# First weight unit and input brought and split in interleaved pieces, in a two-layer hybrid decoder step

## What is computed

```python
x = x + 0.5 * swiglu(rmsnorm(x, norm_ffn1), ffn1_gate, ffn1_up, ffn1_down)
proj = rmsnorm(x, norm_mix) @ w_in        # columns split into 4 head groups
x = x + concat(rwkv7, rglru, gated_delta_net, gla) @ w_out
x = x + 0.5 * swiglu(rmsnorm(x, norm_ffn2), ffn2_gate, ffn2_up, ffn2_down)
```

## Time and profile before

| what | value |
|---|---|
| median of three timed runs | 1355.63 us (1355.2 to 1355.84) |
| profiled execution, first to last instruction (span) | 1353.3 us |
| TensorE busy | 1328.3 us, 98% of the span |
| VectorE busy | 855.3 us, 63% |
| ScalarE busy | 692.1 us, 51% |
| granted TensorE clock, mean of the core | 0.999 |
| first matmul | 7.46 us after the span's start |

### The profile page before, as it was taken

The page is one execution under the profiler, slowest core; times in us unless marked ns, Lnnn a source line. Parts: engine busy times, 40 slices in busy tenths (PEclk is TensorE's granted clock), DMA queues, the critical chain, the costliest instruction groups (busy, mean ns, idle before and its releaser), DMA issues.

```text
span 1353.3 us, 31424 instructions
## 1 busy us (share of the span) xinstructions
PE 1328.3 (98%) x12584; PEld 1288.1 (95%) x12584; DVE 855.3 (63%) x1327; ACT 692.1 (51%) x995; POOL 77.6 (6%) x113
## 2 busy tenths in 40 slices
PE   7999999999999999999999999999999999999997
PEld 7999999998888999999999999999888899999997
DVE  6656533898876756653376555349988767555533
ACT  6554423757565654443365444347466655444423
POOL 0000000200030100000010000001001310000001
PEclk9999999999999999999999999999999999999999
DMA  8544455322313644444455444443222244544541
GB/s 294 175 147 147 148 155 151 114 79 80 112 50 110 203 153 142 153 155 145 150 189 154 154 141 154 145 151 109 80 79 97 66 158 155 155 148 146 155 141 54
DMA packets 50769, 185.90 MB, mean 137 GB/s; under 512 B 5761, under 2 KB 6273, under 8 KB 50177
## 3 DMA queue, kind: packets, MB, share of 16 engines
q1 hardware_dynamic: 49104, 177.37, 41.5%
q10 hardware_dynamic: 1584, 7.35, 1.5%
HBM read 180.14 MB, written 4.56 MB: 136 GB/s over the span
## 4 chain that ended last, share of the span: by engine, by line
PE 83%; DVE 11%; ACT 3%; issue 2%; DMA 1%; POOL 0%; DVEq 0%; ACTq 0%; POOLq 0%
PE ps L479 26%; PE ps L481 25%; PE ps L480 25%; DVE wl L1592 2%; DVE ar L1749 2%; PE ps L847 1%; DVE ar L1663 1%; PE ps L749 1%; DMA raw<-wts 1%; PE ps L1035 0%; PE ps L1013 0%; DVE ar L1740 0%; ACT ar L1299 0%; ACT wh L1186 0%; PE ps L817 0%
## 5 line engine op out<-in xcount | busy, mean ns | idle before, releaser
L479 PE MATMUL ps<-xh,wh 128*128 128x320 f32 x1952 | 611.2, 313 | 8.2 <-DVE xl L1614 8.2
L1592 DVE TENSOR_TENSOR wl<-raw,wh 128x1024 fp32r<-128x1024 f32 x332 | 407.9, 1230 | 318.1 <-ACT wh L1186 317.8
L481 PE MATMUL ps<-xh,wl 128*128 128x320 f32 x1952 | 603.8, 309 | 0.0
L480 PE MATMUL ps<-xl,wh 128*128 128x320 f32 x1952 | 603.8, 309 | 0.0
L1186 ACT ACTIVATE wh<-raw 128x1024 fp32r<-128x1024 f32 x332 | 349.1, 1054 | 355.6 <-PE ps L481 339.0
L479 PEld LDWEIGHTS ps<-xh,wh 128*128 128x128 f32 x1952 | 367.0, 188 | 19.1 <-issue 9.0
L480 PEld LDWEIGHTS ps<-xl,wh 128*128 128x128 f32 x1952 | 367.2, 188 | 0.5
L481 PEld LDWEIGHTS ps<-xh,wl 128*128 128x128 f32 x1952 | 367.1, 188 | 0.0
L479 PE MATMUL ps<-hid_h,wh 128*128 (+1 forms) x704 | 217.5, 309 | 0.0
L480 PE MATMUL ps<-hid_l,wh 128*128 (+1 forms) x704 | 217.5, 309 | 0.0
L481 PE MATMUL ps<-hid_h,wl 128*128 (+1 forms) x704 | 217.5, 309 | 0.0
(11 more groups left out here) (290 smaller groups left out, 935.2 us busy)
## 6 DMA issues: line engine op xcount, KB each, us to landing
raw<-wts SPq DMA_DIRECT2D x332, 512.0 KB, 3.5
ms<-mst ACTq DMA_DIRECT2D x2, 1440.0 KB, 7.6
mout<-ms ACTq DMA_DIRECT2D x2, 1440.0 KB, 6.6
x<-xT SPq DMA_DIRECT2D x4, 320.0 KB, 4.8
yT<-x SPq DMA_DIRECT2D x4, 320.0 KB, 2.5
cs<-cst SPq DMA_DIRECT2D x1, 652.0 KB, 8.0
pr<-par ACTq DMA_DIRECT2D x1, 429.0 KB, 4.3
pr<-par ACTq DMA_DIRECT2D x1, 425.0 KB, 5.2
```

The costliest lines, as they stand in the source:

```text
L479: pe.matmul(out, a, rh, start=start, stop=False)
L480: pe.matmul(out, a, rl, start=False, stop=False)
L481: return pe.matmul(out, b, rh, start=False, stop=stop)
L1592: tt(wl[:, s, :], raw_of(layer, n), wh[:, s, :].bitcast(F32), ALU.subtract).then_inc(lo_ready.sem, 1)
```

## The change

The first weight unit is brought in two transfers (columns 0 to 255, then the rest) and split in three pieces (columns 0 to 255, 256 to 511, 512 to 1023), which stand among the tiles of the input on ScalarE and VectorE. The input comes in transfers of one, one, two and four tiles. TensorE's wait for `lo_ready` of unit 0 moves from its first block to its fifth. The first weight piece counts on the semaphore of the gains (`norms_in`), which ScalarE now awaits ahead of its first activation.

```diff
+        X_PIECES = (slice(0, 1), slice(1, 2), slice(2, 4), slice(4, 8))
...
             def load_x(s):
-                sp.dma_start(x[:, 2 * s:2 * s + 2, :], xT[:, 2 * s:2 * s + 2, :]).then_inc(x_in[s].sem, 16)
+                k = X_PIECES[s]
+                sp.dma_start(x[:, k, :], xT[:, k, :]).then_inc(x_in[s].sem, 16)
...
-            load(0)
-            for s in range(4):
-                load_x(s)
+            sp.dma_start(raw[:, 0, 0:256], wts[0, :, 0:256]).then_inc(norms_in.sem, 16)
+            load_x(0)
+            load_x(1)
+            sp.dma_start(raw[:, 0, 256:], wts[0, :, 256:]).then_inc(raw_in[0].sem, 16)
+            load_x(2)
+            load_x(3)
             load(1)
...
-                    if k == 0:
+                    if k == (0 if m else KT // 2):
                         pe.wait_ge(lo_ready.sem, layer * UNITS + base + m + 1)
...
-                split_hi(0, 0)
-                act.wait_ge(norms_in.sem, 16)
+                def first_hi(lo, hi):
+                    return act.activation(wh[:, 0, lo:hi], raw[:, 0, lo:hi], ACT.Copy)
+
+                act.wait_ge(norms_in.sem, 32)
+                first_hi(0, 256)
                 for k in range(KT):
-                    act.wait_ge(x_in[k // 2].sem, 16)
+                    if k == 2:
+                        act.wait_ge(raw_in[0].sem, 16)
+                        first_hi(256, 512)
+                    if k == 4:
+                        first_hi(512, 1024).then_inc(hi_ready.sem, 1)
+                    for s, piece in enumerate(X_PIECES):
+                        if k == piece.start:
+                            act.wait_ge(x_in[s].sem, 16)
                     act.activation(xh[:, k, :], x[:, k, :], ACT.Copy, scale=P("n1", k)).then_inc(xh_ready.sem, 1)
...
+                def first_low():
+                    for k in range(KT):
+                        ve.wait_ge(xh_ready.sem, k + 1)
+                        if k in (0, 2, 4):
+                            cols = slice(128 * k, 1024 if k == 4 else 128 * k + 256)
+                            if k == 4:
+                                ve.wait_ge(hi_ready.sem, 1)
+                            ins = tt(wl[:, 0, cols], raw[:, 0, cols], wh[:, 0, cols].bitcast(F32), ALU.subtract)
+                            if k == 4:
+                                ins.then_inc(lo_ready.sem, 1)
+                        stt(xl[:, k, :], x[:, k, :], P("n1", k), xh[:, k, :].bitcast(F32), ALU.mult, ALU.subtract).then_inc(xl_ready.sem, 1)
+
                 if layer == 0:
-                    split_lo(layer, 0)
-                    norm_low(layer, 0, "n1")
+                    first_low()
```

## The result

| | before | changed |
|---|---|---|
| median of 21 runs | 1354.94 us (1353.5 to 1356.37) | 1356.79 us (1354.82 to 1359.08) |
| profiled execution, span | 1353.3 us | 1355.1 us |

The ratio is 1.0012 (95% interval 1.0007 to 1.0018): the changed kernel is slower by 1.6 us, 0.9 to 2.4. That is less than 0.2%, but not no difference, and its sign is the opposite of the forecast one. With more runs the median before also lies 0.7 us under the one of three runs that the prediction started from.

A forecast was written before the change was run, and what follows sets the result against it. The prediction took TensorE's unbroken stretch of matmuls to bound the kernel. Unit 1 starting at 12.31 instead of 12.87 us wins 0.56 us, other effects cost nothing: 1355.63 - 0.56 = 1355.1 us, range 1353.9 to 1356.6.

The forecast's parts named there:

- What bounds the kernel: Whole execution: TensorE busy 98%, unbroken from its first matmul; only bringing that stretch forward helps, at most part of 7.46 us.
- First matmul at 5.7 to 6.7 us: TensorE's start: needing only a quarter unit, gains and tile 0, it begins 0.8 to 1.8 us sooner than 7.46.
- So the last byte of the input lands when it did: 2.60 + 5.3 = 7.9 us: Input load: same bytes ahead, engines at about 410 GB/s without a pause, so the landing time stays unchanged.
- slower transfers: Rival, loads at the start: shorter rows at half of 410 GB/s delay unit 1 by 1.1 us, 1356.2 us; chance 0.08.
- The chain from the landing: ScalarE and VectorE splits after input lands at 7.90 us: unit 1 starts on TensorE at 12.31 instead of 12.87.
- The clock: Rival, TensorE's start: holes keep the clock low, 1.75 us lost, 1356.8 us; chance 0.15.
- -0.56 as forecast: Start of unit 1 on TensorE: 12.31 us instead of 12.87, 0.56 us won for the whole execution.
- 0.03 for "slower": Whole kernel: chance 0.03 of measurably slower, from low clock and slow transfers together or an unseen program shift.
- The size against the whole: Whole kernel's time: every case stays within 0.2%, 2.7 us, told as no change; chance 0.95.
- The direction: Whole kernel's time: likeliest case is faster, 1355.63 to 1355.1 us; chance 0.62.

The follow-up runs named there:

- transfers-only runs: Changed kernel's transfers kept, unit 0 split whole ahead of the tiles as before; against the kernel before 1.0021 (first try, late table load) and 1.0014 (remade).
- the three variants: Changed kernel with input in four two-tile transfers (1.0003), first unit in one transfer (1.0005, then 0.9998), or tiles 0 and 1 issued from ScalarE's queue (1.0005).
- two queues: Changed kernel with input tiles 0 and 1 issued from ScalarE's queue instead of SP's; 1.0005 against the kernel before.
- holes filled: Changed kernel with 16 matmuls of zeros in each of its two holes, none ahead of the first matmul; 1.0032, again 1.002, against the kernel before.
- changed, filled: Changed kernel with 36 matmuls of zeros ahead of its first matmul and 16 in each of its two holes; 1.0015 against the kernel before.
- splits only: Changed kernel's splits in pieces, but unit 0 in one transfer and input in pairs as before; 0.9999 against the kernel before, in both tries.
- five fills: Matmuls of zeros added to the changed kernel (1.0015; holes alone 1.0032, 1.002), the kernel before (1.0011) and splits in pieces with the old transfers (1.0011).

## Why the prediction was wrong

*What bounds the kernel*: right. TensorE has no hole from the 25th matmul to 240 us, and that matmul is 1.75 us late for 1.6 us (0.9 to 2.4) by the medians. That the two profiled spans differ by 1.8 us as well is partly luck, since the spans of the changed kernel alone run from 1353.0 to 1357.3 us.

*First matmul at 5.7 to 6.7 us*: it came at 5.1. The chain of 1.9 us held; what it starts from, the gains and the first piece, was there at 3.15 instead of 4.75 us.

*"So the last byte of the input lands when it did: 2.60 + 5.3 = 7.9 us"*: **this step failed.** It landed at 9.5. The step took the 410 GB/s of the earlier trace rows for a property of the engines, whatever is queued. They were measured with 320 to 512 KB per issue of 0.47 us; with the 128 to 160 KB per issue of the change, which the issue rate holds to at most 160 KB / 0.47 us = 350 GB/s by this estimate, 245 GB/s flowed from 2.6 to 4.2 us for 396 before. The step also kept the issue time of before, 2.60 us, though the last input transfer is now sixth in the queue and issued at 3.08. I had slower transfers as a rival and priced them at 1.1 us, but looked for the cause in row length, which costs some 0.13 us, and gave it 0.08. The transfers-only runs show that the arrangement of the transfers makes the input late, and the three variants that larger transfers early in the queue, or a sooner issue of the large ones, mend it.

Of the 1.55 us, lost flow explains a part: 0.19 MB missing at 5 us is 0.5 us at 400 GB/s. The rest is unevenness. The semaphore of the last input transfer counts 16 arrivals. They came from 7.4 to 7.9 us before and from 7.9 to 9.5 after, 15 of the 16 by 8.7; in the second profile of the changed kernel 15 had come by 8.4 and the last at 9.9. Over all profiles the 16 spread over 0.6 to 1.4 us without changed transfers and over 1.6 to 2.4 us with them. So most of the delay is in a few late arrivals. Why these fall behind stays open; a dip in the flow is not enough, since in two queues, with its dip from 2.6 to 3.0 us, the spread is 1.2 us.

*The chain from the landing*: right in form. From landing to the 25th matmul I summed 12.31 - 7.90 = 4.41 us. With the high clock it takes 4.36 (holes filled) and 4.35 (changed, filled).

*The clock*: the other rival, 0.15, came true beside the first. In the changed kernel the way from the landing to the 25th matmul is 5.14 us, 0.7 over the sum: unit 0's last blocks still ran at 0.27 us. My argument against it, that the holes are below a microsecond, failed: they were 1.3 and 1.1 us. The first of them, ahead of tile 2, I had not listed; tiles 2 and 3 landed at 6.8 us, and TensorE had been through with tile 1 since 7.1. In the table's ten profiles without a fill and with holes of at most 0.3 us until the pace changed, it changed 2.8 to 5.5 us after the first matmul; in the changed kernel's two profiles it did after 9.4 and 12.1 us. By the rule of the Trainium skill (TensorE: Matmul & The Clock Gate, Part 1), that the clock is released by sustained activity and that the observation runs freely, the moment differs between executions and moves with holes; these profiles agree with it. That holes put the change off rests on the two profiles of the changed kernel and on one with the holes filled (3.75 us after the first matmul); in the second profile of that the fill was too short, and it changed after 9.4 us.

The sum of both: -0.56 as forecast, +1.6 from the landing, +0.7 from the clock, together 1.75 us later, as the profile shows. The -0.56 was not measured by itself; the nearest is splits only, with the landing of before and its 25th matmul 0.4 us sooner than before. Both rivals together stood in the prediction only as a part of the 0.03 for "slower", which asked for more than came.

*The size against the whole*: within 0.2%, as forecast. The direction was wrong, and the median lies 0.2 us above the range.

## What to carry over

A transfer rate read from a profile holds for the queue as it was: before cutting a load at the head of a program into small pieces, divide their bytes by the time of one issue, and look at when the large ones behind them are issued; here small ones cost nothing that could be measured behind a large one. Look at the last of the 16 arrivals too, not only at GB/s. A start that comes earlier but with holes can end later, since an unbroken stretch begins when its last input has come. Look at where the first long stretch without a wait begins, not at the first matmul. And when waits are moved on ScalarE, look at where the table load stands. A trick that brings the clock up sooner has to be timed over the whole program: here none of the five fills made the whole faster.

## What else the runs showed

The clock also falls in the middle of the program, in some executions and not in others. The changed kernel in the second layer's mixing stage:

```profile
996.00:1000.80 4.80, 4.29 (x53) 3.35 (x52) 3.18 (x6) 4.62 (x9) 0.00 (x0) 1.00 0.51 132
1000.90:1004.20 3.30, 3.30 (x15) 3.30 (x14) 1.76 (x3) 3.25 (x5) 0.00 (x0) 0.50 0.33 129
```

In the first profile of the kernel before the same window shows 1.00; in its second the clock falls to 0.50 there too, from 997.4 us on. From the norm's matmul to the end, profiles without a fill differ by 2.5 us, more than the whole effect studied here, so a change of 0.1% is told from none only by the start of the timeline and by many runs together.
